# A bidirectional recurrence on one core: one transposition and one small product moved in between the Gram products

## The reference, cut to what matters

```python
def rwkv7_step(state, inp):
    r, w, k, v, kk, a = inp
    sa = jnp.einsum('...vk,...k->...v', state, -kk)
    state = (state * w[..., None, :]
             + sa[..., :, None] * (kk * a)[..., None, :]
             + v[..., :, None] * k[..., None, :])
    y = jnp.einsum('...vk,...k->...v', state, r)
    return state, y
...
    wl = jnp.tanh(wl.reshape(bsz, seq, 2, DECAY_LORA))
    w_log = -jax.nn.softplus(-(w0 + jnp.einsum('btdr,drc->btdc', wl, w2))) - 0.5
    decay = jnp.exp(-jnp.exp(w_log.astype(jnp.float32)))
    a = jax.nn.sigmoid(a0 + jnp.einsum('btdr,drc->btdc', al.reshape(bsz, seq, 2, ICLR_LORA), a2))
```

## Time and profile before

| | us, or a number of records |
|---|---|
| median of 3 runs (lowest, highest) | 1748.77 (1746.99, 1751.68) |
| the profiled execution, its own time | 1745.65 |
| its span in the trace | 1743.9 |
| PE busy in the span | 1690.4 (97%) |
| PE matmuls in the span | 12,773, as many weight loads |
| DVE, ACT, POOL busy | 1044.2 (60%), 815.2 (47%), 457.6 (26%) |
| start of the Gram products of pair 0, 1, 2, 3 | 153.27, 197.75, 245.11, 290.91 |
| first step of the chain after pair 3 | 340.89 |

### The profile page before, as it was taken

One profiled execution on the slowest core, in us unless ns is written; L12 is line 12 of the kernel. 1 busy time (PEld: TensorE's weight loads), 2 busy tenths in 40 slices (PEclk: granted clock), 3 DMA queues, 4 the chain that ended last, 5 costly groups with the idle time before them and its releaser, 6 DMA issues.

```text
span 1743.9 us, 29667 instructions
## 1 busy us (share of the span) xinstructions
PE 1690.4 (97%) x12773; PEld 1385.1 (79%) x12773; DVE 1044.2 (60%) x1308; ACT 815.2 (47%) x1237; POOL 457.6 (26%) x407
## 2 busy tenths in 40 slices
PE   7999899899999999999999999999999999999999
PEld 6878788778888787888887886668887788788887
DVE  5478677356343666766675455975434455685667
ACT  5254555536553433543355236865654343453344
POOL 2002322220100472245310220540010166114620
PEclk9999999999999999999999999999999999999999
DMA  7210000243222565365443222003431275356534
GB/s 255 85 48 2 4 5 6 73 169 123 95 97 73 202 233 181 126 245 183 163 169 108 97 75 71 1 2 121 145 108 41 94 264 196 132 195 239 196 102 155
DMA packets 116925, 212.70 MB, mean 122 GB/s; under 512 B 4247, under 2 KB 50938, under 8 KB 116794
## 3 DMA queue, kind: packets, MB, share of 16 engines
q1 hardware_dynamic: 103239, 159.59, 27.2%
q0 software_dynamic: 13264, 51.09, 8.2%
q10 hardware_dynamic: 291, 0.12, 0.0%
HBM read 185.62 MB, written 25.17 MB: 121 GB/s over the span
## 4 chain that ended last, share of the span: by engine, by line
PE 74%; DVE 11%; ACT 6%; issue 3%; POOL 3%; DMA 3%; SPq 0%; DVEq 0%; ACTq 0%; POOLq 0%
PE PS L431 50%; PE PS L538 10%; POOL DW L671 2%; DVE WLO L397 1%; ACT WHI L386 1%; PE PS L1929 1%; DVE SS L2237 1%; PE PS L1898 1%; DMA WRAW<-ab_w_in 1%; PE PS L937 1%; DMA diff_dn<-DW 1%; PE PS L1379 1%; DVE AT L2249 1%; DVE SQN L1013 1%; PE PS L2068 1%
## 5 line engine op out<-in xcount | busy, mean ns | idle before, releaser
L397 DVE TENSOR_TENSOR WLO<-WRAW,WHI 128x2048 fp32r<-128x2048 f32 (+1 forms) x106 | 249.1, 2361 | 296.0 <-ACT WHI L386 296.0
L431 PE MATMUL PS<-HIS,WHI 128*128 128x512 f32 x856 | 334.6, 391 | 4.8 <-DVE LOS L2412 2.1
L431 PE MATMUL PS<-LOS,WHI 128*128 128x512 f32 x856 | 333.1, 389 | 0.0
L431 PE MATMUL PS<-HIS,WLO 128*128 128x512 f32 x856 | 333.1, 389 | 0.0
L386 ACT ACTIVATE WHI<-WRAW 128x2048 fp32r<-128x2048 f32 (+1 forms) x107 | 203.0, 1907 | 229.0 <-PE PS L431 181.6
L431 PE MATMUL PS<-WHI,HIS 128*128 128x512 f32 x608 | 240.4, 395 | 1.1 <-DVE LOS L728 1.1
L431 PE MATMUL PS<-WLO,HIS 128*128 128x512 f32 x608 | 236.9, 390 | 0.0
L431 PE MATMUL PS<-WHI,LOS 128*128 128x512 f32 x608 | 236.7, 389 | 0.0
L431 PEld LDWEIGHTS PS<-HIS,WHI 128*128 128x128 f32 x856 | 160.7, 188 | 42.4 <-issue 5.7
L431 PEld LDWEIGHTS PS<-HIS,WLO 128*128 128x128 f32 x856 | 160.7, 188 | 33.5
L431 PEld LDWEIGHTS PS<-LOS,WHI 128*128 128x128 f32 x856 | 160.7, 188 | 32.9
(11 more groups left out here) (327 smaller groups left out, 2844.3 us busy)
## 6 DMA issues: line engine op xcount, KB each, us to landing
WRAW<-ffn_w_up SPq DMA_DIRECT2D x88, 512.0 KB, 4.9
RW<-ffn_w_down POOLq DMA_DIRECT2D x22, 1024.0 KB, 7.3
diff_dn<-DW POOLq DMA_DIRECT2D x22, 1024.0 KB, 5.3
WRAW<-cross_wkv SPq DMA_DIRECT2D x16, 1024.0 KB, 5.0
PW<-diff_dn SPq DMA_DIRECT2D x8, 1536.0 KB, 9.3
WRAW<-diff_w_in SPq DMA_DIRECT2D x12, 1024.0 KB, 5.1
WRAW<-ab_w_in SPq DMA_DIRECT2D x10, 1024.0 KB, 5.7
PW<-diff_dn SPq DMA_DIRECT2D x8, 1280.0 KB, 7.5
```

The lines of the kernel that those rows point to most:

```text
L397: V.e.tensor_tensor(part(WLO[place(i)], i), part(WRAW[raw_slot[i]], i), part(WHI[place(i)], i).bitcast(F32), ALU.subtract).then_inc(S("w_l ...
L431: mm = e.matmul(o, l, r, start=(si == 0 and kk == 0 and q == 0), stop=(si == len(steps) - 1 and kk == nk - 1 and q == 2))
```

## The change

Three pieces of work are moved; none is added or left out.

- The transposition of BET to tokens goes from place 6 (level 3) to between the two BET groups of the Gram products, and from banks 6 and 7 to banks 2 and 3, where the states of the previous pair have been. ScalarE's copy of it into GB (now in `gram_act`) goes to the start of the pair's list.
- The first half of the next pair's low-rank product goes from place 3 (end of level 1) to between the two KAP groups of the Gram products, into banks 2 and 3 as well; its tanh stands behind the copy into GB. In the last pair place 3 keeps the gates' products, as before.
- The waits follow: the transposition waits for the banks (`p_qfree`), the low-rank product for the copy, the second direction of level 0's first product for the tanh (in the last pair for the copy). The order in `p_tok` becomes BET, AR, KAP.

```diff
@@ -1194,6 +1194,12 @@
                           start=True, stop=True)
         mm.then_inc(S("p_lora"), 1)
 
+    def tokens_pe(e, l, b0):
+        for d in range(2):
+            for t in range(NT):
+                mm = e.transpose(PS[:, b0 + d, t * P:t * P + P], l[:, d, t * P:t * P + P], ident)
+        mm.then_inc(S("p_tok"), 1)
+
     def gram_pe(T, j):
         e = T.e
         ar = AR[j % 2]
@@ -1212,12 +1218,19 @@
         mm.then_inc(S("p_a"), 1)
 
         for l, d, b in ((BET, 0, 6), (BET, 1, 0), (KAP, 0, 4), (KAP, 1, 6)):
+            if l is BET and d == 1:
+                if j > 0:
+                    e.wait_ge(S("p_qfree"), j)
+                else:
+                    e.wait_ge(*at("zu", "ev", 4))
+                tokens_pe(e, BET, 2)
+            if l is KAP and d == 1 and j + 1 < NJ:
+                e.wait_ge(S("p_tokfree"), 3 * j + 1)
+                lora_pe(e, j + 1, 0, 2)
             if l is KAP:
                 e.wait_ge(S("p_afree" if d == 0 else "p_bfree"), 2 * j + (2 if d == 0 else 1))
             elif j > 0:
                 e.wait_ge(S("p_yfree" if d == 0 else "p_pfree"), j)
-            elif d == 1:
-                e.wait_ge(*at("zu", "ev", 4))
             for t in range(NT):
                 for hh in range(2):
                     for x in range(2):
@@ -1268,15 +1281,12 @@
             e.wait_ge(S("p_gfree"), 2 * (j + 1))
             e.wait_ge(S("p_bonus"), j + 1)
             e.matmul(PS[:, 6, :], rk("bones"), TMP[1][:, 0, :], start=True, stop=True).then_inc(S("p_bonmm"), 1)
-        elif s == 3:
-            e.wait_ge(S("p_bonfree"), j + 1)
-            if j + 1 < NJ:
-                lora_pe(e, j + 1, 0, 6)
-            else:
-                gates_pe(e, 0)
+        elif s == 3 and j + 1 == NJ:
+            e.wait_ge(S("p_bonfree"), NJ)
+            gates_pe(e, 0)
         elif s == 4:
             if j + 1 < NJ:
-                e.wait_ge(S("p_lorafree"), 2 * j + 3)
+                e.wait_ge(S("p_bonfree"), j + 1)
                 lora_pe(e, j + 1, 1, 6)
             else:
                 e.wait_ge(S("f_gg"), 2)
@@ -1294,12 +1304,9 @@
                         mm = e.transpose(PS[:, 6 + hh, (d * NT + t) * HD:(d * NT + t) * HD + HD],
                                          AR[j % 2][half(hh), d, 0, t * P:t * P + P], KC[half(hh), HD * hh:HD * hh + HD])
             mm.then_inc(S("p_tok"), 1)
-        elif s in (6, 7):
-            e.wait_ge(S("p_tokfree"), 3 * j + s - 5)
-            for d in range(2):
-                for t in range(NT):
-                    mm = e.transpose(PS[:, 6 + d, t * P:t * P + P], (BET, KAP)[s - 6][:, d, t * P:t * P + P], ident)
-            mm.then_inc(S("p_tok"), 1)
+        elif s == 7:
+            e.wait_ge(S("p_tokfree"), 3 * j + 2)
+            tokens_pe(e, KAP, 6)
         elif s == 8:
             e.wait_ge(S("p_tokfree"), 3 * j + 3)
             if j == 0:
@@ -1325,8 +1332,11 @@
                 e.wait_ge(S(f"p_u{d}"), j * (LV + 1) + lv + 1)
                 if lv == 0 and d == 0:
                     e.wait_ge(S("p_bfree"), 2 * j + 2)
-                if lv == 0 and d == 1 and j > 0:
-                    e.wait_ge(S("p_qfree"), j)
+                if lv == 0 and d == 1:
+                    if j + 1 < NJ:
+                        e.wait_ge(S("p_lorafree"), 2 * j + 3)
+                    else:
+                        e.wait_ge(S("p_tokfree"), 3 * j + 1)
                 if lv == 0:
                     for u in range(8):
                         for x in range(2):
@@ -1504,29 +1514,25 @@
             e.wait_ge(S("p_bonmm"), j + 1)
             e.activation(BON[j][:, :], PS[:, 6, :], ACT.Copy).then_inc(S("p_bonfree"), 1)
         elif s in (3, 4):
-            if j + 1 < NJ:
-                prep_tanh_act(e, j + 1, s - 3, 6)
-            else:
+            if s == 4 and j + 1 < NJ:
+                prep_tanh_act(e, j + 1, 1, 6)
+            elif j + 1 == NJ:
                 fin_gate_act(e, 2 * s - 6)
                 fin_gate_act(e, 2 * s - 5)
         elif s == 5:
-            e.wait_ge(S("p_tok"), 3 * j + 1)
+            e.wait_ge(S("p_tok"), 3 * j + 2)
             for d in range(2):
                 i = e.activation(units(AXT[:, d, :, 0:HD]),
                                  banks2(6, d * 256, 256).rearrange("p b (t k) -> p b t k", k=HD), ACT.Copy)
             i.then_inc(S("p_tokfree"), 1)
-        elif s in (6, 7):
-            e.wait_ge(S("p_tok"), 3 * j + s - 4)
+        elif s == 7:
+            e.wait_ge(S("p_tok"), 3 * j + 3)
             for d in range(2):
-                if s == 6:
-                    i = e.activation(units(GB[:, d, :, CH:P]), PS[:, 6 + d, :].rearrange("p (t b k) -> p b t k", b=2, k=HD),
-                                     ACT.Copy)
-                else:
-                    i = e.activation(KPD[:, d, :, :], PS[:, 6 + d, :].rearrange("p (t k) -> p t k", k=P), ACT.Copy)
+                i = e.activation(KPD[:, d, :, :], PS[:, 6 + d, :].rearrange("p (t k) -> p t k", k=P), ACT.Copy)
             i.then_inc(S("p_tokfree"), 1)
-            if s == 7 and j + 1 < NJ:
+            if j + 1 < NJ:
                 prep_exp_act(e, j + 1)
-            elif s == 7:
+            else:
                 e.wait_ge(S("p_bet"), NJ)
                 hi_part(A)
         elif s == 9 and j + 1 == NJ:
@@ -1542,8 +1548,17 @@
         e.wait_ge(S(f"p_tn{d}"), j * (LV - 1) + lv)
         e.activation(TT[:, d, :, :], PS[:, 4, :].rearrange("p (u k) -> p u k", k=CH), ACT.Copy).then_inc(S(f"p_t{d}"), 1)
 
+    def gram_act(e, j):
+        e.wait_ge(S("p_tok"), 3 * j + 1)
+        for d in range(2):
+            i = e.activation(units(GB[:, d, :, CH:P]), PS[:, 2 + d, :].rearrange("p (t b k) -> p b t k", b=2, k=HD), ACT.Copy)
+        i.then_inc(S("p_tokfree"), 1)
+        if j + 1 < NJ:
+            prep_tanh_act(e, j + 1, 0, 2)
+
     def pair_act(A, j):
         e = A.e
+        gram_act(e, j)
         for lv in range(LV):
             if lv > 0:
                 turn_u_act(e, j, lv, 0)
```

## The result

The changed kernel took 1752.03 us (median of 21 runs, 1749.63 to 1760.04), the kernel before 1748.60 beside it (21 runs, 1744.34 to 1756.15). The ratio is 1.0024 [1.0013, 1.0035], about 4.2 us slower by it and 3.4 by the medians: inside the 0.3% that the prediction counted as no change, and 1.0 us above the predicted 1751.0. In a later job one run of the kernel before took 5981.52 us; it is left out of all ratios.

What follows compares the result with a forecast made beforehand. TensorE's instruction list was taken to bound the kernel. The terms summed to +0.2, +1.4, +0.7 and +0.1 us in pairs 0 to 3, together +2.4 on 1748.77, giving 1751.2, or 1751 us; range 1745 to 1757.

Steps and rivals of the forecast that it cites:

- part four: Level 3: GpSimd's earlier first BET step delays VectorE's second scan; +1.2 us in pair 1, +0.5 in pair 2.
- part one: Gram products: the inserted transposition and low-rank half lengthen them by 1.7, 1.3, 1.2 and 0.45 us in pairs 0 to 3.
- part two: Place 3, end of level 1: without the low-rank half, 1.06 us comes back in each of pairs 0, 1 and 2.
- Part three: Place 6, level 3: the 0.87 us of transposition stays as waiting; the copy into GB goes, giving back 0.4 us.
- No meeting: Rival: GpSimd starts after the second scan or yields; level 3 gains 0.4 us in all pairs; 1748.7 us, chance 0.16.
- Cover: Rival: packets and masks hold up the Gram products enough that inserted work is free; -4.8 us, 1744.0, chance 0.12.
- No cover: Rival: halts stay as long; 1.93 us added in full, 0.87 in pair 3; +4.4 us, 1753.2, chance 0.12.
- Shared reading in full: Rival: in level 3 of pairs 1 and 2 the 2.25 us delay reaches TensorE unabsorbed; +5.2 us, 1754.0, chance 0.18.

Runs made afterwards that it cites:

- a1_again: The changed kernel once more, unaltered, beside new runs of the kernel before on another chip: 1752.84 us, ratio 1.0019.
- e1: The changed kernel with GpSimd's first BET step held back until level 3's first transposition of UU, near its old time: 1748.97 us, ratio 1.0003 to the kernel before.
- c0_same: The kernel before, unchanged, run once more as a control: 1747.85 us, ratio 1.0004.
- e3: The kernel before with only the low-rank half moved, to between the two KAP groups: 1746.15 us, ratio 0.9988.
- e5: The kernel before with only the low-rank half moved, to between the two BET groups: 1745.63 us, ratio 0.9972.
- e6: The kernel before with only BET's transposition moved (order BET, AR, KAP) and GpSimd's first BET step held to its old start: 1748.84 us, ratio 0.9992.

## Why the prediction was right, and where its sizes were off

The sum was +2.4 us and the mechanism that of part four; at one clock +3.1 ± 0.6 were measured, in the medians 3.4. That the sum came so near is in part luck: the Gram products (part one) came out 0.5 us above their terms in the profile of after and 1.6 above in a1_again's, and place 3 (part two) gave back 1.1 more than its terms. By its steps:

**Part one** (Gram products, +1.7, +1.3, +1.2, +0.45): from A to level 0 they got longer by 1.75, 1.48, 1.23 and 0.70 us, and in a1_again by 1.76, 1.75, 1.77 and 0.98. Right in kind and low in most pairs; by how much depends on the halts of the execution, and only pair 0, without a halt, repeats. In pair 1 of after, counted as the forecast did from the end of the halt, it is 1.76, and of the 0.46 too much 0.15 is the transposition (1.02 instead of 0.87 between groups of another shape), 0.40 the four groups, less the 0.09 of halt that was left over in the forecast. In pair 2 the forecast counted 67 records behind the halt where 70 stood (6 BET, 64 KAP), which moves it by less than 0.1. The halt of 0.84 in pair 2's BET groups is gone in after, and 0.23 of it is left in a1_again, near the 0.2 forecast. The states' tail ahead of these groups halts in all of them; in pair 3 of after the halt is still inside, at 1.09. Before (pair 2's tail), after (the same, then pair 3) and a1_again (pair 2), timeline, PE:

```profile
244.98 0.34 PE L1419 MATMUL PS<-VTK,KPD 64*64 64x64 f32 x6 [1.36 <-issue]
...
249.82 0.34 PE L1429 MATMUL PS<-VTK,KPD 64*64 64x64 f32 x6 [1.33 <-issue]
...
298.45 0.43 PE L1237 MATMUL PS<-AR,BET 64*64 64x128 f32 x2 [1.09 <-issue]
...
252.04 0.56 PE L1237 MATMUL PS<-AR,BET 64*64 64x128 f32 x12 [0.23 <-issue]
```

**Part two** (place 3, -1.06 in pairs 0 to 2): level 1 is shorter by 1.06, 1.81 and 1.38. In pair 0 that is the term itself. In pair 1 a halt went as well (0.52 us at 211.68 of before), and in pair 2 62 records of L1337 take 1.03 us instead of 1.28. That the moved work shifted the ends of the packets would explain both; no run tests it. The term was too small.

**Part three** (level 3, -0.4 without a meeting): where no meeting is (pair 3, and pair 1 of e1), level 3 is shorter by 0.44, and the 0.87 us of transposition came back as 0.69 of waiting for TT, as forecast. In pair 0 it was 0.17.

**Part four** (the meeting): L1665 started 1.02 us after GpSimd's work before it, while the first scan ran, and the second took 3.31 us (3.3 forecast). The forecast put level 3 of pair 1 at 1.6 us above its value without the meeting, and 1.5 was measured. In pair 2 it put 0.9, and 1.5 was measured: the mis-sized term. There I counted 1.9 us of slack for XX, and part of that was a halt of before, which is in neither profile of the changed kernel (timeline of before, PE):

```profile
269.81 0.34 PE L1337 MATMUL PS<-UU,AI 64*64 64x64 f32 x6 [0.43 <-issue]
```

The 62 records of that product take 1.80 us to the next start, 1.03 in pair 1. Without these 0.77 us the slack is 1.1, that of pair 1, and the price is the same. Against before itself level 3 of pair 2 is only 0.31 longer (7.32 and 7.01), where +0.5 was forecast, since the halt went at the same time. And what is late first is not XX, which the forecast named, but the step of the chain, whose YL stands ahead of XX on VectorE and ahead of both second products on TensorE; pair 2 shows the same as pair 1 (POOL, then DVE, then PE):

```profile
272.57 2.94 POOL L1665 TENSOR_TENSOR BET<-KK,TMP 128x1024 f32<-128x1024 f32 x1 [1.02 <-PE PS L1304]
```

```profile
273.28 3.32 DVE L1610 TENSOR_TENSOR_SCAN TMP<-RC,TMP 128x512 f32<-128x512 f32 x1
```

```profile
277.03 0.45 PE L1254 MATMUL PS<-QT,PT 64*64 64x64 f32 x8 [1.06 <-DVE YL L1270]
```

The Trainium skill ("SBUF — State Buffer", section "SBUF: two separate sides") says that VectorE, with two SBUF inputs, and GpSimd share a pair of ports by an exclusive lock that whoever starts first holds for its whole instruction. The 3.31 us agree: GpSimd, whose step takes 2.93 us here and 2.37 in e1, ends 2.14 after the first scan, and the second scan ends 1.09 after GpSimd, about the 1.20 that it takes without the meeting.

**The rivals.** "No meeting" gave 1748.7 for a kernel that e1 then was: 1748.97. "Cover" (-4.8) failed in pair 0, as its argument against said. "No cover" (+4.4) lies outside the +3.1 ± 0.6 and forecast 0.87 for pair 3 and 1.93 for each of the others, where 0.70 to 0.98 and 1.23 to 1.77 were measured; in pairs 1 and 2 of a1_again it is not far off. "Shared reading in full" (+5.2) would have wanted 2.65 in each pair instead of 1.5.

**What stays open.** The sum over the pairs, from A of pair 0 to the end of pair 3's states, doesn't follow the runs as closely as the single steps do. It is 186.39 us in before's profile and 185.99 in c0_same's. In after's it is 188.02 and in a1_again's 190.82, each with one stretch at half the clock inside: pair 0's tail takes 10.59 instead of 9.14, pair 1's level 3 8.62 instead of 7.32. Less these excesses the changed kernel is 0.2 us longer than before in one profile and 3.1 in the other, and their halts differ by 2.5 us (7.7 and 10.2). What sets the halts of an execution isn't known. In e1 the sum is 184.52, 1.9 less than before's, and its runs are not faster (+0.2 ± 0.7); in e3 it is 2.6 less, and 1.2 in the runs. All that lies outside the pairs took 0.8 and 0.9 us longer in these profiles than in that of before, at work that the edits don't touch, and the rest of the gap is not explained.

## What to carry to other kernels

A wait on a count means "the n-th of these", so whoever changes the order of the increments changes what every untouched waiter waits for: look at each of them, and at what the earlier start will run beside. Work put into a stretch with halts of this kind can fill one, if it stands ahead of it (0.8 of 1.06 us in pair 2 of e5, none in e3), but halts can come up again behind it, so only the time of the whole tells what the place is worth (-2.0 ± 0.7 and -1.2 ± 0.7 us here, which don't differ beyond noise). A piece that hides a round trip between two engines (BET's transposition between the two turns of UU) was worth nothing in its new place (+0.2 ± 0.7 us in e6), since the round trip stays, as 0.69 us of waiting for TT. And one profile of a kernel is not enough where its halts vary from execution to execution.

## What the runs showed of the hardware that was not expected

Each kernel here had runs with a mean granted clock under 1.00, in a program that is 97% busy on TensorE, and where a profile caught it, it was a matter of stretches of some microseconds at half the clock. After the pairs both kernels halt for the same time ahead of the chain's step. Timeline of after, PE (before has 1.23 us at 340.89, and its first L431 takes 0.50):

```profile
344.94 0.65 PE L1254 MATMUL PS<-QT,PT 64*64 64x64 f32 x8 [1.24 <-issue]
345.32 0.70 PE L1259 MATMUL PS<-RT,QT 64*64 64x64 f32 x8
345.94 0.79 PE L431 MATMUL PS<-WHI,HIS 128*128 128x512 f32 x1
```

The same halt was followed by the full clock in one execution and by a stretch of 0.66 in the other. The 21 runs of before lie up to 11.8 us apart, more than three times the effect of the change. In the 63 runs of before whose clocks are on record, the spread (standard deviation) falls from 3.4 to 1.2 us when they are put to one clock. So for differences of a few microseconds the mean clock of each run is to be read beside its time.
